# Seven block products for eight in the second MLP matmul of a two-layer decoder step

## The reference

```python
def squared_relu_mlp(x, w1, w2):
    h = jax.nn.relu(x @ w1)
    return (h * h) @ w2
x = layer_norm(ALPHA * x + squared_relu_mlp(x, w1, w2), g, b)
```

## Time and profile before

| | us |
|---|---|
| median of 3 runs | 1247.8 (1246.69 to 1247.99) |
| profiled execution, its own time | 1249.62 |
| its span, first to last instruction | 1247.6 |
| PE busy | 1199.7 (96%), 9582 matmuls |
| DVE busy | 708.1 (57%) |
| ACT busy | 477.1 (38%) |
| mean granted clock of PE | 0.992 of 2.4 GHz |

### The profile page before, as it was taken

How to read it: one execution, slowest core, us unless ns; L and a number is a source line. 1 busy time by engine, 2 the same in 40 slices (tenths; PEclk the granted TensorE clock), 3 DMA queues, 4 the chain that set the end, 5 groups by cost and what they waited for, 6 DMA issues and landing times.

```text
span 1247.6 us, 25437 instructions
## 1 busy us (share of the span) xinstructions
PE 1199.7 (96%) x9582; PEld 1106.5 (89%) x9582; DVE 708.1 (57%) x1456; ACT 477.1 (38%) x873; POOL 82.5 (7%) x117
## 2 busy tenths in 40 slices
PE   8998988899999999999999999999999999999995
PEld 4958854589999999999999987798999999999994
DVE  2289899857843442443457767678533433433477
ACT  2342166634531331322334566644422322412332
POOL 4434300100030000000000000000000000000000
PEclk9999999999999999999999999899999999999998
DMA  6698580233122222222223211131222222222222
GB/s 208 189 286 264 163 234 2 72 117 102 51 85 100 86 87 99 84 100 85 88 100 107 80 55 51 52 136 35 85 85 92 93 85 101 84 88 97 85 85 69
DMA packets 61960, 129.97 MB, mean 104 GB/s; under 512 B 7819, under 2 KB 34603, under 8 KB 61755
## 3 DMA queue, kind: packets, MB, share of 16 engines
q1 hardware_dynamic: 47899, 115.16, 27.5%
q10 hardware_dynamic: 10624, 7.21, 2.0%
q0 software_dynamic: 3360, 6.56, 1.7%
HBM read 124.36 MB, written 9.79 MB: 108 GB/s over the span
## 4 chain that ended last, share of the span: by engine, by line
PE 81%; DVE 14%; ACT 2%; issue 2%; DMA 0%; SPq 0%; DVEq 0%; ACTq 0%
PE PS L616 61%; PE PS L648 7%; PE PS L1034 3%; PE PS L846 2%; PE PS L793 2%; PE PS L806 2%; DVE YA L1658 2%; PE PS L820 2%; DVE YA L1645 1%; DVE PB L1796 1%; DVE RSTD L1650 1%; DVE SC L1955 1%; DVE MX L1953 1%; DVE X L1664 1%; DVE PB L1821 1%
## 5 line engine op out<-in xcount | busy, mean ns | idle before, releaser
L1501 DVE TENSOR_TENSOR WLO<-WRAW,WHI 128x1024 fp32r<-128x1024 f32 x118 | 145.3, 1231 | 322.2 <-ACT WHI L1096 322.2
L1096 ACT ACTIVATE WHI<-WRAW 128x1024 fp32r<-128x1024 f32 x126 | 133.4, 1059 | 387.4 <-PE PS L616 351.6
L616 PE MATMUL PS<-XH,WHI 128*128 128x260 f32 x1184 | 241.5, 285 | 0.9 <-DVE XL L1828 0.7
L616 PE MATMUL PS<-XH,WLO 128*128 128x260 f32 x1184 | 239.1, 284 | 0.0
L616 PE MATMUL PS<-XL,WHI 128*128 128x260 f32 x1184 | 238.6, 283 | 0.0
L616 PE MATMUL PS<-HH,WHI 128*128 128x260 f32 x944 | 191.2, 284 | 0.2 <-DVE HL L1525 0.2
L616 PE MATMUL PS<-HH,WLO 128*128 128x260 f32 x944 | 190.2, 283 | 0.0
L616 PE MATMUL PS<-HL,WHI 128*128 128x260 f32 x944 | 189.9, 283 | 0.0
L616 PEld LDWEIGHTS PS<-XH,WHI 128*128 128x128 f32 x1184 | 183.1, 189 | 6.4 <-issue 5.4
L616 PEld LDWEIGHTS PS<-XH,WLO 128*128 128x128 f32 x1184 | 183.0, 189 | 0.0
L616 PEld LDWEIGHTS PS<-XL,WHI 128*128 128x128 f32 x1184 | 182.7, 189 | 0.0
(11 more groups left out here) (293 smaller groups left out, 1868.8 us busy)
## 6 DMA issues: line engine op xcount, KB each, us to landing
WRAW<-wall SPq DMA_DIRECT2D x168, 512.0 KB, 3.2
bias_skewed<-bias_seq SPq DMA_DIRECT2D x4, 1280.0 KB, 17.6
BT<-bias_skewed ACTq DMA_DIRECT2D x3, 1024.0 KB, 8.8
X<-xT SPq DMA_DIRECT2D x4, 520.0 KB, 7.0
X<-xT SPq DMA_DIRECT2D x1, 2080.0 KB, 11.1
yT<-X SPq DMA_DIRECT2D x8, 260.0 KB
KVB<-cacheK SPq DMA_DIRECT2D x16, 128.0 KB, 3.2
KVX<-cacheK SPq DMA_DIRECT2D x16, 128.0 KB, 3.2
```

Source lines behind the costliest of these rows:

```text
L616: mm = pe.matmul(PS[:, 2 * slot + g, 0:TG], w[:, slot, k, :], x[:, k, TG * g:TG * g + TG], start=(k == 0 and w is WHI and x is hi), stop=( ...
L1096: nc.scalar.activation(WHI[:, slot], WRAW[:, slot], ACT.Copy).then_inc(hi_done, 1)
L1501: V.tensor_tensor(WLO[:, slot], WRAW[:, slot], WHI[:, slot].bitcast(F32), ALU.subtract).then_inc(lo_dve, 1)
```

## The change

In chunks 0, 1 and 2 the second half is computed by Strassen's identity in Winograd's form. The 1024 x 1024 block of w2 is seen in pairs: for a pair p of output tiles (2p and 2p + 1) the weights are four blocks of 512 x 128: A11, A12 (k-tiles 0 to 3 and 4 to 7 of the even tile, slot 0) and A21, A22 (of the odd tile, slot 1). The hidden values are four blocks too: k-tiles 0 to 3 or 4 to 7 by lower or upper token half. Eight block products become seven, with sums of weight blocks (S1 = A21 + A22, S3 = A11 - A21, S2 = S1 - A11, S4 = A12 - S2) and of hidden blocks (T, written as HHX and HLX). A block product is 4 k-tiles x 3 matmuls of 260 columns into one bank, in turn over the eight banks; each has its own running sum in SBUF (two halves of YA's tiles and SUM1, SUM6, SUM7). The order is A11, S1, S3, A12, S4, A22, S2; in the first pair the last k-tile of S3 and A12 comes behind the first three of both.

- DVE makes the weight sums (128 x 512, into SRAW) and the low parts of seven blocks (128 x 512) a pair, and takes each product from its bank (128 x 260, ev_dve or acc). ACT makes seven high parts of 128 x 512. High and low parts of the seven blocks have one buffer each (RNH, RNL), which lie where BT is.
- For hidden tiles m < 4 of these chunks the square goes to HRAW, and a subtraction (128 x 260) comes before HH. For m >= 4 there are three DVE operations of 128 x 260 (two of them waited for by DVE itself, `after`), and ACT and DVE write HHX and HLX (128 x 780).
- The four sums and the first lows of pair 0 stand ahead of tiles 6 and 7 in the queues of ACT and DVE.
- In chunk 0 ACT writes ALPHA*X32 into YA (start_sums, 128 x 1040, four times) behind the tiles m < 4, and DVE subtracts four halves (128 x 260) ahead of tile 4. In chunk 3 DVE combines the running sums behind each tile.
- BT's second half is loaded again (ACT's queue) in chunk 3 of layer 0, and POOL's additions wait for that. Some unused semaphores are dropped, to make room for new ones. The loops of ACT and DVE over units are written out.
- wait_product waits for a product's semaphore: prod for the blocks in OWN, unit_done for A12 and A22.

Cut to its core, indented less:

```diff
+SEVEN = CHUNKS - 1
+A11, S1, S3, A12, S4, A22, S2 = range(7)
+OWN = {A11: 1, S1: 2, S3: 3, S4: 4, S2: 5}
+SUMS = {S1: 1, S3: 2, S2: 3, S4: 4}
+class Sevens:
+    def __init__(self, base, layer, c):
+        self.c, self.layer = c, layer
+        self.g = SEVEN * layer + c
+        self.first = base + 16 * c + 8
+    def pair(self, p):
+        return 4 * self.g + p
+    def count(self, p, block):
+        return 5 * self.pair(p) + OWN[block]
+    def unit(self, p, block):
+        return self.first + 2 * p + (block == A22)
+    def bank(self, p, block):
+        return (7 * p + block) % 8
+    def bank_user(self, p, block):
+        n = 7 * p + block - 8
+        return None if n < 0 else (n // 7, n % 7)
...
-pool.wait_ge(ev_dve, 16)
+pool.wait_ge(bt_back, 16)
...
-    def second_half(c):
-        two(c * 16 + 8, HH, HL, hidden_there(c))
-        with pe.Fori(1, 4) as i:
-            two(c * 16 + i * 2 + 8, HH, HL)
+    layer = hbase // 32
+    def sevens(c):
+        sv = Sevens(base, layer, c)
+        ev = ev_base + 16 * c
+        lower, upper = slice(0, TG), slice(TG, TOK)
+        operand = {A11: (HH[:, 0:4, lower], HL[:, 0:4, lower]),
+                   S1: (HH[:, 0:4, upper], HL[:, 0:4, upper]),
+                   A12: (HH[:, 4:8, lower], HL[:, 4:8, lower]),
+                   S4: (HH[:, 4:8, upper], HL[:, 4:8, upper]),
+                   S3: (HHX[:, 0], HLX[:, 0]), S2: (HHX[:, 1], HLX[:, 1]),
+                   A22: (HHX[:, 2], HLX[:, 2])}
+        def weights_there(p, block):
+            if block in OWN:
+                pe.wait_ge(blk_lo, sv.count(p, block))
+            else:
+                pe.wait_ge(lo_dve, sv.unit(p, block) + 1 - LO_SKIP)
+        def bank_there(p, block):
+            user = sv.bank_user(p, block)
+            if user is None:
+                if block in (A11, S3):
+                    pe.wait_ge(ev_dve, ev + (7 if block == A11 else 8))
+            elif user[1] in OWN and user[1] != S2 or user[1] == A12:
+                pe.wait_ge(acc, 5 * sv.pair(user[0]) + user[1] + 1)
+            else:
+                pe.wait_ge(ev_dve, ev + 8 + 2 * user[0] + (1 if user[1] == A22 else 2))
+        def hidden_block(p, block, k):
+            if p:
+                return
+            if block == A11 and k == 0:
+                pe.wait_ge(hl_done, c * 8 + hbase + 4)
+            elif block in (A12, S4):
+                pe.wait_ge(hl_done, c * 8 + hbase + 5 + k)
+            elif block in (S3, A22, S2):
+                pe.wait_ge(tl_done, 4 * sv.g + k + 1)
+        def product(p, block, ks):
+            hi, lo = operand[block]
+            at, bank = block, sv.bank(p, block)
+            if ks[0] == 0:
+                weights_there(p, block)
+                bank_there(p, block)
+            for k in ks:
+                hidden_block(p, block, k)
+                for w, x, first in ((RNH, hi, True), (RNH, lo, False),
+                                    (RNL, hi, False)):
+                    mm = pe.matmul(PS[:, bank, 0:TG], w[:, at, k, :], x[:, k, :],
+                                   start=(first and k == 0), stop=(k == 3 and w is RNL))
+            if ks[-1] == 3:
+                mm.then_inc(prod if block in OWN else unit_done, 1)
+        whole = (0, 1, 2, 3)
+        for p in range(4):
+            product(p, A11, whole)
+            product(p, S1, whole)
+            if p == 0:
+                product(p, S3, (0, 1, 2))
+                product(p, A12, (0, 1, 2))
+                product(p, S3, (3,))
+                product(p, A12, (3,))
+            else:
+                product(p, S3, whole)
+                product(p, A12, whole)
+            product(p, S4, whole)
+            product(p, A22, whole)
+            product(p, S2, whole)
...
-    second_half(0)
-    with pe.Fori(1, CHUNKS - 1) as c:
+    sevens(0)
+    for c in range(1, SEVEN):
         first_half(c, 0)
-        second_half(c)
+        sevens(c)
...
+    layer = base // MLP1
+    def next_unit(u):
+        act.wait_ge(raw_in[u % 2], 16 * (u // 2 + 1))
+        high_part(None, u % 2)
+    def rectify(c, m):
+        u = base + 16 * c + m
+        src = quad_banks(m) if c == 0 and m < 4 else banks(m % 2)
+        act.wait_ge(unit_done, u + 1)
+        if m < 6 and not (c == 0 and m < 4) or c == SEVEN:
+            next_unit(u + 2)
         nc.scalar.activation(RL[:].rearrange("p (g t) -> p g t", g=2),
                              src, ACT.Relu).then_inc(relu_done, 1)
+        act.wait_ge(ev_dve, ev_base + 16 * c + m + 1)
+    def hidden(c, m):
+        rectify(c, m)
+        nc.scalar.activation(HH[:, m, :], S32[:], ACT.Copy).then_inc(hh_done, 1)
+    def hidden_sevens(c, m):
+        g = SEVEN * layer + c
+        rectify(c, m)
+        if m < 4:
+            act.wait_ge(t_raw, 8 * g + m + 1)
+            nc.scalar.activation(HH[:, m, :].rearrange("p (g t) -> p g t", g=2),
+                                 HRAW[m][:, 0:2, :], ACT.Copy).then_inc(hh_done, 1)
+        else:
+            nc.scalar.activation(HH[:, m, :], S32[:], ACT.Copy).then_inc(hh_done, 1)
+            act.wait_ge(t_raw, 8 * g + m + 1)
+            nc.scalar.activation(HHX[:, :, m - 4, :], TRAW[:], ACT.Copy
+                                 ).then_inc(ht_done, 1)
+    def start_sums(k):
+        act.wait_ge(x_new, 8 * n + 8)
+        act.wait_ge(x_odd, 8 * n + 8)
+        nc.scalar.activation(YA[:, k:k + 2, :], X32[:, k:k + 2, :], ACT.Copy,
+                             scale=float(ALPHA)).then_inc(ya_init, 1)
+    def block_high(sv, p, block):
+        if p:
+            wait_product(act, sv, p - 1, block)
+        if block in SUMS:
+            act.wait_ge(s_sum, 4 * sv.pair(p) + SUMS[block])
+            src = SRAW[:, (SUMS[block] - 1) % 2]
+        else:
+            u = sv.unit(p, block)
+            act.wait_ge(raw_in[u % 2], 16 * (u // 2 + 1))
+            src = WRAW[:, u % 2, 0:4] if block == A11 else WRAW[:, u % 2, 4:8]
+        nc.scalar.activation(RNH[:, block], src, ACT.Copy
+                             ).then_inc(blk_hi if block in OWN else hi_done, 1)
+    for c in range(SEVEN):
+        sv = Sevens(base, layer, c)
+        for m in range(8):
+            if m == 6:
+                block_high(sv, 0, A11)
+                block_high(sv, 0, S1)
+            if m == 7:
+                block_high(sv, 0, S3)
+                block_high(sv, 0, A12)
+            hidden_sevens(c, m)
+            if c == 0 and m < 4:
+                start_sums(2 * m)
+        for block in (A22, S4, S2):
+            block_high(sv, 0, block)
+        for p in range(1, 4):
+            for block in (A11, S1, A12, S3, A22, S4, S2):
+                block_high(sv, p, block)
+        next_unit(base + 16 * c + 16)
+        next_unit(base + 16 * c + 17)
+    for m in range(8):
+        hidden(SEVEN, m)
+        if m == 4 and layer == 0:
+            act.wait_ge(comb, 4)
+            act.dma_start(BT[:, :, 256:512], bskew[:, :, 127 + 256:127 + 512]
+                          ).then_inc(bt_back, 16)
+    act.wait_ge(comb, 8 * layer + 8)
...
+    layer = sq0 // 32
+    halves = (slice(0, TG), slice(TG, TOK))
+    def square(c, m, out):
+        src = quad_banks(m) if c == 0 and m < 4 else banks(m % 2)
+        if sq0 + 8 * c + m:
+            dve.wait_ge(hl_done, sq0 + 8 * c + m)
+        dve.wait_ge(relu_done, sq0 + 8 * c + m + 1)
+        V.tensor_tensor(out, RL[:].rearrange("p (g t) -> p g t", g=2),
                         src, ALU.mult).then_inc(ev_dve, 1)
+    def hidden_low(c, m, src):
+        dve.wait_ge(hh_done, sq0 + 8 * c + m + 1)
+        V.tensor_tensor(HL[:, m, :].rearrange("p (g t) -> p g t", g=2), src,
+                        HH[:, m, :].bitcast(F32).rearrange("p (g t) -> p g t", g=2),
+                        ALU.subtract).then_inc(hl_done, 1)
+    def next_low(c, m):
+        if m < 6 and not (c == 0 and m < 4) or c == SEVEN:
+            low_part(base + 16 * c + m + 2, m % 2)
+    s32 = S32[:].rearrange("p (g t) -> p g t", g=2)
+    def hidden_sevens(c, m):
+        g = SEVEN * layer + c
+        if m < 4:
+            h = HRAW[m]
+            square(c, m, h[:, 0:3:2, :])
+            dve.wait_ge(ev_dve, ev_base + 16 * c + m + 1)
+            V.tensor_tensor(h[:, 1, :], h[:, 2, :], h[:, 0, :], ALU.subtract
+                            ).then_inc(t_raw, 1)
+            hidden_low(c, m, h[:, 0:2, :])
+            return
+        h = HRAW[m - 4]
+        square(c, m, s32)
+        dve.wait_ge(ev_dve, ev_base + 16 * c + m + 1)
+        if 4 * g + m - 4:
+            dve.wait_ge(tl_done, 4 * g + m - 4)
+        after(V.tensor_tensor(TRAW[:, 0, :], S32[:, halves[1]], h[:, 2, :],
+                              ALU.subtract))
+        after(V.tensor_tensor(TRAW[:, 1, :], TRAW[:, 0, :], h[:, 0, :], ALU.add))
+        V.tensor_tensor(TRAW[:, 2, :], S32[:, halves[0]], TRAW[:, 1, :],
+                        ALU.subtract).then_inc(t_raw, 1)
+        hidden_low(c, m, s32)
+        dve.wait_ge(ht_done, 4 * g + m - 3)
```

(123 more changed lines are left out.)

108 lines of the change are left out of this document (26 added, 82 removed).

## The result

The changed kernel takes **1261.15 us** (median of 4, 1259.9 to 1262.82), the one before 1247.89 (4 runs beside it, 1246.69 to 1248.62). The ratio is **1.0114**, 95% interval 1.0095 to 1.0134: 1.1% slower, where 0.3% was forecast. In the profiled executions it is 1261.81 against 1249.62, or +12.2 us for the forecast's +3.9. Experiments are compared by such ratios, each to the kernel before on its own chip. Of the four runs of one experiment (the additions later, alone, told under 6) two had a mean granted clock of 0.85 and 0.56 and are left out, so that it has only a profiled execution of 1255.74 and a run of 1257.5.

A forecast was written before the change was run, and what follows sets the result against it. PE alone was taken to set the pace in both MLP layers. Terms -34.6 + 5.4 + 12.0 - 0.6 + 9.8 + 10.2 + 1.7 = +3.9 gave 1251.7 us; own range 1245 to 1258, 8 in 10 1238 to 1263.

The forecast's parts named there:

- rival 3: Clock falls at all six hand-overs, costing 10.2 us in place of 1.7: 1260 us; chance 0.15.
- Matmuls: Second halves of chunks 0 to 2, both layers: 288 fewer matmuls on PE at 0.120 us each, -34.6 us.
- First units: Chunk 0, tiles 0 to 3: longer ACT and DVE turns delay units 4, 5, 6 by 2.7 us a layer, +5.4.
- Hand-over of chunks 1 and 2: PE stalls at the first products because DVE's queue is late: 3.0 us, four times, +12.0.
- Hand-over of chunk 0: Starts later behind start_sums and subtractions; PE stalls 4.9 us, twice, 3.4 of it before S3: +9.8.
- Pairs: Colliding weight loads make the odd slot's loop 10.6 to 11.0 us against PE's 10.1: 1.7 us, six times, +10.2.
- The upper end: Upper bound for the pairs' cost: 3 us per chunk if weight loads take 5 us.
- Clock: Chunk 0's 3.4 us gap drops the clock once a layer, losing 1.7 us, half lying in the following wait: +1.7.
- At no cost: End combination, BT's reload, two loads and POOL's 13.6 us of additions beside the last chunk's hidden tiles: nothing, or 0.5 us.
- the old waits: Chunk 0's present hand-over stall of 0.2 to 0.5 us goes: -0.6 us for two layers.
- Rival 1: Weight loads don't collide and DVE catches up in the pairs; the 10.2 shrinks to 1 or 2: 1243 us; chance 0.27.
- rival 2: Hand-overs are cheap as DVE's 260 and 512 operations overlap more; half of 27 us goes: 1238 us; chance 0.08.

The follow-up runs named there:

- the additions later, alone: Changed kernel with only POOL's 16 mask additions moved behind the low part of layer 0's last hidden tile: profiled 1255.74 us, one run 1257.5.
- told under 6: Changed kernel with ACT's first sums between relu and the square's wait, and POOL's additions behind layer 0's last hidden tile: 1249.44 us, ratio 1.0016.
- Experiment 5: Changed kernel with one 260-column DVE subtraction instead of three operations in hidden tiles 4 to 7, so three products compute other values: 1248.32 us, ratio 1.0022.
- Experiment 9: Every block product four PSUM banks further, against the kernel with sums in the gap, additions later and three raw-weight places (1233.53 us): 1240.21 us, ratio 0.9948.
- experiment 1: Changed kernel with POOL's sixteen mask additions one column wide instead of 256, leaving out most of the mask: 1254.9 us, ratio 1.0081.
- experiments 2 and 7: Two runs on the changed kernel: experiment 2, and 7, with three places for the second halves' raw weights, loads full-sized: 1243.61 us, ratio 0.9982.
- experiment 2: Changed kernel with half-sized weight loads in the second halves of chunks 0 to 2, the rest being old data: 1247.3 us, ratio 1.0006.
- experiment 3: Changed kernel with 24 extra matmuls into an idle bank before chunk 0's first S3, so PE doesn't idle there: 1260.39 us, ratio 1.012.

## Why the prediction was right, and where its sum was off

The sign held, and so did the mechanism in the main: matmuls are saved at 0.12 us each, and PE waits for DVE at the hand-overs and for late weights in the pairs. The median lies in the range of 8 in 10 (1238 to 1263), but outside the forecast's own, 1245 to 1258: it was let in by the room made for rival 3 (1260), which did not happen, and that much is luck. PE's idle time in the two MLPs, waits over 0.15 us counted from start to start (without the wider spacing of matmuls at the low clock), is 22.3 + 17.8 = 40.1 us; before it was 1.0. That is 39 us for the 38 in the forecast's summary, against -34.6 of matmuls. This agreement too is in part luck, as the terms show:

- *Matmuls, -34.6:* 288 fewer, at 0.12 us. Held, one bank twelve times in a row included.
- *First units, +5.4:* waits of 1.54 + 1.07 + 0.61, and 1.64 + 1.04 + 0.61, make 6.5. The first two are 0.1 to 0.5 over their 1.1 and 0.9, the last 0.1 under its 0.7.
- *Hand-over of chunks 1 and 2, +12.0:* 11.9, and each of the three waits was 0.0 to 0.2 from its size. Experiment 5 confirms the cause. Experiment 9 corrects how the text put it: "1.4 at S3, whose bank waits" reads like a price of the bank, while it is one lateness that PE meets wherever it waits first.
- *Hand-over of chunk 0, +9.8:* 3.4 us in one piece, to the tenth, twice, but the 1.1 and 0.5 behind it didn't come. While the clock was low, DVE caught up with them; in experiment 1, where it stayed up, they came. With the clock's term the forecast had 11.5 us for these two hand-overs; it was 6.8 of idle time and 1.7 + 3.0 of slow matmuls (next but one), 11.5. The two parts were each off by 3, and cancelled.
- *Pairs, +10.2:* mis-sized, and the loop that was walked is not the one that bound. The forecast has the odd slot, A22's low, the load, sum S1, "sum S1 waiting for WRAW in pairs 2 and 3". In the trace S1 waits only in pair 1, six times, 6.5 us in all. In pairs 2 and 3 it is the even slot: A12's low, the load, A11's high and low part, which stand ahead of S1 in ACT's and DVE's order. A11's high part waits in ten of these twelve pairs, for loads of 3.4 to 4.9 us, and a round takes 10.3 to 11.9 us where 10.6 to 11.0 were forecast. The first unit of the next chunk waits 0.75 to 0.83, not 0.5. The waits over 0.15 us in the pairs make 11.3. With the smaller ones the term is 14: the six chunks of the change are 8.6 us longer than before, and with the other terms taken off 14.2 are left, beside the 15.5 and 14.7 that experiments 2 and 7 took out of the same six. The upper end, 3 us per chunk, would have been 18.
- *Clock, +1.7:* one fall per layer was right for layer 0's S3 (0.61 and 0.54 in the windows at 368 and 370), 1.7 us of slow matmuls. Layer 1's was longer, 0.85 at 920, 0.50 in the three windows to 928 and 0.94 in the next; PE started again at 922.28, so it lost half of 6.0 us, 3.0. A third one stood where none was forecast, in the windows from 648 to 652, behind POOL's 2.35 us: some 1.3.
- *At no cost:* this is **the step that failed**, "POOL's 13.6 us of additions, now beside the last chunk's hidden tiles; without that cover, 0.5 us as now". The price looked up was that of another place, where DVE's waiting hid the slowdown. The slowdown itself stood in the forecast's own lines: HL beside the additions took 1.14 us where its kind takes 0.71. Beside tiles whose DVE work had just grown by the combination the additions cost 3.6 us of idle PE and 1.3 of slow matmuls, 4.9 by the stretch from layer 0's last hidden tile to layer 1's first; experiment 1 took out 4 us (0.33%, by the intervals 0 to 8) and 5.0 by that stretch, the additions later 5.1 by it. The reload of BT and the combination itself did cost nothing.

The gap of the sum, 12.2 - 3.9 = 8.3 us, is then: 1.1 in the first units, -0.1 in the hand-overs of chunks 1 and 2, -3.0 in chunk 0's, 3.0 for its clock, 4.0 in the pairs, 4.9 for POOL with its clock, -0.4 because all 1.0 us of the old waits went, not 0.6, and -1.2 ahead of layer 0's MLP, which the change doesn't touch. (The pairs' term is what the others leave of the six chunks, so this sum can't fail there; experiments 2 and 7 are its check.)

*Rival 1* (the loads don't collide) fell with the landings of up to 5.24 us and experiment 2, *rival 2* with the three waits. *Rival 3* (the clock falls at all six hand-overs) did not happen: three waits of 1.46, 0.82 and 0.20 us within 5 us left the clock at 1.00 in all of chunks 1 and 2. But its mechanism is real, and near: experiment 9 merges the same waits, and four of six hand-overs fall. The Trainium skill ("TensorE: Matmul & The Clock Gate", A second HAM failure mode: psum-queue depth-cycling) has the clock going back and forth from short idles between groups of matmuls as PSUM banks are cycled. Here the traces differ: the short idles, 2.5 us of them in all, left the granted clock at 1.00, and the same time in one piece let it fall in four of six places.

## What to carry to other kernels

Saving an engine's work pays only if the engines that feed it have the time at the moment when it is due; here their busy shares (73% and 43%) looked easy, and PE still waited 40 us, because the extra work was stacked in front of one hand-over and because a buffer was freed late and needed first. Look for such loops (freed by, loaded, read by) and break them with memory that is idle in that stage, and keep POOL's additions away from any stretch in which DVE is close behind. When several waits of one engine have a single cause, removing the first one moves the time to the next, and merging them can cost more than it did spread out.

## What the runs showed of the hardware that was not expected

- POOL's additions and DVE's operations take turns, but not with every operation. Beside 16 additions of 128 x 256, DVE's operations with both inputs in SBUF take up to 0.55 us longer each, whether of 260, 520 or 1024 columns (0.97 for 0.42, 1.23 for 0.71, 1.75 for 1.23); the square, with one input in PSUM, takes 0.68 as ever. In the single records of the trace an addition takes 0.73 us alone and 0.92, 1.2 or 1.7 beside such an operation of 260, 520 or 1024 columns, and a DVE operation that began ahead of it isn't lengthened. The one of 1024 columns below keeps its 1.23 us, and two additions take 2.40 us together (the additions later, alone):

```profile
648.15 2.40 POOL L662 TENSOR_TENSOR BT<-BT,CST 128x256 f32<-128x256 f32 x2
648.73 1.23 DVE L1879 TENSOR_TENSOR WLO<-WRAW,WHI 128x1024 fp32r<-128x1024 f32 x1 [0.39 <-ACT WHI L1322]
```

  So how much DVE loses depends on how closely its operations follow one another. POOL's sixteen take 13.56 us where DVE has three such operations in that time, 15.59 beside the last chunk's tiles and 19.90 beside the last output tiles. The Trainium skill ("GPSIMD Engine Reference", Specifications) lists the SBUF interface as shared with VectorE, with contention for instructions with two SBUF inputs; the traces agree, by the numbers above.
- The granted clock depends on how idle time is cut up. Gaps of about 1.46, 0.84 and 0.22 us in three pieces: no fall in any of the 36 hand-overs of chunks 1 and 2 that have them (the change and eight experiments). A gap of 2.54 us and 0.22: a fall in four of six. A gap of 3.24 us: a fall in nine of ten, of 3.4 us in five and 6.8 in four. The exceptions differ in nothing that the waits show, so the same gap isn't always met in the same way, and a single profile can't tell what a gap costs.
- A fall of the clock costs little where the engine that PE waits for next is late by as much: the time was the same with it and without (experiment 3), and the one place with the same gap and no fall (experiment 1, layer 0) is 1.0 us shorter.
